# High and low activations side by side: the two matmuls that share weights take 320 and 256 columns instead of 288 and 288

## The reference

```python
h = _rmsnorm(x, norm_mix)
proj = h @ w_in                        # 2048 x 7240: q, k, v, indexer, S5 input u, two gates
attn = _dsa_attend(...)                # indexer scores, top-k, attention over selected keys
y_a = attn @ w_attn_proj
s5_y, new_re, new_im = _s5(u, ...)     # diagonal complex state-space scan
z = jax.nn.gelu(s5_y)
glu_a, glu_g = jnp.split(z @ w_glu, 2, axis=-1)
y_b = glu_a * jax.nn.sigmoid(glu_g)
x = x + (jax.nn.sigmoid(ga) * y_a + jax.nn.sigmoid(gb) * y_b) @ w_out
up = _rmsnorm(x, norm_ffn) @ w_up      # 2048 x 11264, then a causal conv of width 3
x = x + (jax.nn.silu(gate) * val) @ w_down
y = _rmsnorm(x, norm_final)
```

## Time and profile before

| | |
|---|---|
| runs | 1706.43, 1709.63, 1708.58 us; median 1708.58 |
| the profiled execution | 1707.09 us, of which 1705.4 us from the first to the last instruction |
| TensorE matmuls busy | 1622.1 us, 95% of the span, 12814 instructions |
| VectorE busy | 1026.1 us, 60% |
| ScalarE busy | 771.1 us, 45% |
| GpSimd busy | 457.1 us, 27% |
| DMA queues | 274.46 MB, mean 161 GB/s |

### The profile page before, as it was taken

How to read it: one execution, slowest core, us unless ns; L and a number is a source line. 1 busy time by engine, 2 the same in 40 slices (tenths; PEclk the granted TensorE clock), 3 DMA queues, 4 the chain that set the end, 5 groups by cost and what they waited for, 6 DMA issues and landing times.

```text
span 1705.4 us, 35779 instructions
## 1 busy us (share of the span) xinstructions
PE 1622.1 (95%) x12814; PEld 1588.9 (93%) x12814; DVE 1026.1 (60%) x1542; ACT 771.1 (45%) x1082; POOL 457.1 (27%) x650
## 2 busy tenths in 40 slices
PE   6699989889998999999999999999999999999997
PEld 4699879889898999999999999999999999999997
DVE  4574465757465555666677777777777774444441
ACT  4233434455455665343445445445445444333333
POOL 2591256664642332012211111111111112000110
PEclk9799899999999999999999999999999999999998
DMA  7355425445446555755564554554555556555552
GB/s 247 111 146 165 122 81 150 138 126 165 138 141 216 154 163 146 208 168 159 193 197 148 159 185 149 159 183 153 158 181 156 157 179 231 165 166 169 161 170 73
DMA packets 278087, 274.46 MB, mean 161 GB/s; under 512 B 21979, under 2 KB 275031, under 8 KB 276912
## 3 DMA queue, kind: packets, MB, share of 16 engines
q1 hardware_dynamic: 266128, 247.37, 47.7%
q10 hardware_dynamic: 9024, 18.23, 3.1%
q0 software_dynamic: 2848, 7.64, 1.3%
HBM read 259.56 MB, written 13.60 MB: 160 GB/s over the span
## 4 chain that ended last, share of the span: by engine, by line
PE 77%; POOL 6%; DVE 5%; ACT 4%; issue 4%; DMA 1%; ACTq 1%; POOLq 1%; SPq 0%; DVEq 0%
PE banks L417 24%; PE banks L419 24%; PE banks L418 24%; PE banks L425 2%; POOL clam L1630 2%; DVE wlo L1046 2%; ACT tlag L847 1%; POOL wq L1603 1%; DMA raw<-in_w_in 1%; POOL clam L1462 1%; ACT whi L739 1%; DVE sc L1162 1%; DMA scratch_mask<-wks 1%; POOL xb L1652 1%; POOL xs L1662 0%
## 5 line engine op out<-in xcount | busy, mean ns | idle before, releaser
L1046 DVE TENSOR_TENSOR wlo<-raw,whi 128x1024 fp32r<-128x1024 f32 x444 | 554.3, 1262 | 343.0 <-ACT whi L739 337.6
L739 ACT ACTIVATE whi<-raw 128x1024 fp32r<-128x1024 f32 x444 | 462.5, 1052 | 490.5 <-PE banks L419 466.3
L418 PE MATMUL banks<-h_lo,whi 128*128 128x288 f32 x1408 | 415.7, 295 | 0.0
L419 PE MATMUL banks<-h_hi,wlo 128*128 128x288 f32 x1408 | 415.7, 295 | 0.0
L417 PE MATMUL banks<-h_hi,whi 128*128 128x288 f32 x1408 | 414.6, 294 | 0.1
L417 PE MATMUL banks<-hhi,whi 128*128 128x288 f32 (+1 forms) x928 | 283.0, 305 | 20.6 <-DVE wlo L1046 18.6
L419 PE MATMUL banks<-hhi,wlo 128*128 128x288 f32 (+1 forms) x928 | 278.5, 300 | 0.0
L418 PE MATMUL banks<-hlo,whi 128*128 128x288 f32 (+1 forms) x928 | 278.3, 300 | 0.0
L418 PEld LDWEIGHTS banks<-h_lo,whi 128*128 128x128 f32 x1408 | 264.6, 188 | 0.1
L417 PEld LDWEIGHTS banks<-h_hi,whi 128*128 128x128 f32 x1408 | 264.1, 188 | 0.3 <-issue 0.3
L419 PEld LDWEIGHTS banks<-h_hi,wlo 128*128 128x128 f32 x1408 | 264.4, 188 | 0.0
(11 more groups left out here) (355 smaller groups left out, 2432.0 us busy)
## 6 DMA issues: line engine op xcount, KB each, us to landing
raw<-in_w_up SPq DMA_DIRECT2D x352, 256.0 KB, 3.4
raw<-in_w_in SPq DMA_DIRECT2D x224, 256.0 KB, 3.2
raw<-in_w_down SPq DMA_DIRECT2D x176, 256.0 KB, 3.0
raw<-in_w_glu SPq DMA_DIRECT2D x64, 256.0 KB, 2.9
raw<-in_w_out SPq DMA_DIRECT2D x64, 256.0 KB, 3.2
raw<-in_w_attn_proj SPq DMA_DIRECT2D x32, 256.0 KB, 4.1
scratch_gates<-gt ACTq DMA_DIRECT2D x16, 288.0 KB, 3.2
x<-scratch_x_kept ACTq DMA_DIRECT2D x2, 2304.0 KB, 9.2
```

Source lines behind the costliest of these rows:

```text
L418: pe.matmul(out, h, xl[:, kt, :], start=False, stop=False)
L419: mm = pe.matmul(out, lo, xh[:, kt, :], start=False, stop=kt == nk - 1)
L739: act.activation(whi[:, s, :, 0:cols], raw[:, s, :, 0:cols], ACT.Copy).then_inc(hi_ready, 1)
L1046: dve.tensor_tensor(wlo[:, s, :, 0:cols], raw[:, s, :, 0:cols], whi[:, s, :, 0:cols], ALU.subtract).then_inc(lo_ready, 1)
```

## The change

**Layout.** Each pair of buffers becomes one of [128, tiles, 576]: low half in columns 0 to 287, high half in 288 to 575. In a tile the order is then low prompt (256), low samples (32), high prompt (256), high samples (32). Addresses of the whole are as before; `z` tiles are stored rotated by four, because of what else lies there, and read in the same order as before (`k0=4`).

**Matmuls.** The first with the high weights now reads 320 columns, low samples and the whole high half, into columns 0 to 319 of the bank; the second the 256 low prompt columns into 32 to 287; the third, with the low weights, the 288 high columns into 32 to 319. The result (`res`) lies in columns 32 to 319, but the products of the low samples lie apart, in columns 0 to 31 (`extra`).

**VectorE.** Before each use of a group, `add_extra` copies the 2 x 32 extra columns to SBUF (`part`) and adds them to the sample columns of the result, in PSUM; `fold` is `add_extra` with a link behind it. The KIWI group has the same by halves, four instructions.

**GLU gate.** ScalarE's sigmoid of the gate half (L922) read the accumulator by itself, behind `acc_free[0]`; it now waits for `gate_folded`, which VectorE gives after it has waited for the group and added.

```diff
+    part = at("part", [P, 2, TS], F32, 4960)
...
-    hhi = at("hhi", [P, KD, T], F32R, RE)
-    hlo = at("hlo", [P, KD, T], F32R, RE + 18432)
+    hx = at("hx", [P, KD, 2 * T], F32R, RE)
+    hlo, hhi = hx[:, :, 0:T], hx[:, :, T:2 * T]
...
+    res, extra = acc[:, :, TS:TS + T], acc[:, :, 0:TS]
...
-                            out = acc[0:w, 2 * g_parity + m, 0:T]
+                            out = acc[0:w, 2 * g_parity + m, :]
...
-                            pe.matmul(out, h, xh[:, kt, :], start=kt == 0, stop=False)
-                            pe.matmul(out, h, xl[:, kt, :], start=False, stop=False)
-                            mm = pe.matmul(out, lo, xh[:, kt, :], start=False, stop=kt == nk - 1)
+                            xk = x[:, (k0 + kt) % nk, :]
+                            pe.matmul(out[:, 0:TS + T], h, xk[:, TP:2 * T], start=kt == 0, stop=False)
+                            pe.matmul(out[:, TS:TS + TP], h, xk[:, 0:TP], start=False, stop=False)
+                            mm = pe.matmul(out[:, TS:TS + T], lo, xk[:, T:2 * T], start=False, stop=kt == nk - 1)
...
-                    act.wait_ge(acc_free[0], 15 + i)
-                    act.activation(glu_gate[:, :, :], acc[:, 2:4, 0:T], ACT.Sigmoid).then_inc(acc_free[1], 1)
+                    act.wait_ge(sem("gate_folded"), i + 1)
+                    act.activation(glu_gate[:, :, :], res[:, 2:4, :], ACT.Sigmoid).then_inc(acc_free[1], 1)
...
+            def add_extra(parity):
+
+                samples = res[:, 2 * parity:2 * parity + 2, TP:T]
+                own.link(dve.tensor_copy(part[:, :, :], extra[:, 2 * parity:2 * parity + 2, :]))
+                return dve.tensor_tensor(samples, samples, part[:, :, :], ALU.add)
+
+            def fold(parity):
+                own.link(add_extra(parity))
+
             def evac(dst, parity, c_end):
 
                 dve.wait_ge(chunks_used, c_end)
-                dve.tensor_tensor(dst, acc[:, 2 * parity:2 * parity + 2, 0:T], bc(rstd[:, :], 1, 2), ALU.mult).then_inc(acc_free[parity], 1)
+                fold(parity)
+                dve.tensor_tensor(dst, res[:, 2 * parity:2 * parity + 2, :], bc(rstd[:, :], 1, 2), ALU.mult).then_inc(acc_free[parity], 1)
...
+                    dve.wait_ge(chunks_used, c + 2)
+                    add_extra(1).then_inc(sem("gate_folded"), 1)
                     lo(c, 4)
```

More of the change, by code:

```diff
@@ L401, in _, with group @@
         def _(pe):
-            def group(g_parity, use, c, nk, xh, xl, widths=(P, P), before={}, slot0=0):
+            def group(g_parity, use, c, nk, x, widths=(P, P), before={}, slot0=0, k0=0):
                 if not (isinstance(use, int) and use == 0):
@@ L452, in _ @@
             mm.then_inc(sem("rb_ready"), 1)
[L453 to L460, removed]
+            group(1, 0, C_U + 4, KD, hx)
+            group(0, 1, C_U + 8, KD, hx)
+            group(1, 1, C_U + 12, KD, hx)
+            group(0, 2, C_KIWI, KD, hx, widths=(P, IH))
+            group(1, 2, C_QI, KD, hx)
+            group(0, 3, C_QI + 4, KD, hx)
+            group(1, 3, C_KV, KD, hx)
+            group(0, 4, C_KV + 4, KD, hx)
             for r in range(4):
@@ L572, in gates @@
                 more = it < N_GATE - 1
[L573 to L574 removed]
+                group(1, 6 + it, c, KD, hx, before={0: (lambda: chunk_inputs(it),), 2: ahead})
+                group(0, 7 + it, c + 4, KD, hx, before={0: (lambda: powers_t(it + 1, 0),), 1: (lambda: powers_t(it + 1, 1),),
                                                               2: (lambda: lag_kernels(it + 1),)} if more else {})
@@ L654, in unit @@
                     start = ()
-                group(1, 14 + i, c, 8, zhi, zlo, before={0: start, 1: middle})
-                group(0, 15 + i, c + 2, 8, zhi, zlo, slot0=2, before={0: (lambda: prompt_probs(i),),
+                group(1, 14 + i, c, 8, zx, k0=4, before={0: start, 1: middle})
+                group(0, 15 + i, c + 2, 8, zx, slot0=2, k0=4, before={0: (lambda: prompt_probs(i),),
                                                                       1: (lambda: prompt_values(i), lambda: sample_probs(i))})
@@ L1095, in evac_blocks @@
                 dve.wait_ge(chunks_used, C_U + 4 * k + 4)
+                fold(k % 2)
                 for i in range(4):
@@ L1120, in _ @@
             dve.wait_ge(chunks_used, C_KIWI + 4)
-            dve.tensor_tensor(kiT[:, :], acc[:, 0, 0:T], rstd[:, :], ALU.mult)
-            dve.tensor_tensor(wiT[:, :], acc[0:IH, 1, 0:T], rstd[0:IH, :], ALU.mult).then_inc(acc_free[0], 1)
+            own.link(dve.tensor_copy(part[:, 0, :], extra[:, 0, :]))
+            own(dve.tensor_tensor(res[:, 0, TP:T], res[:, 0, TP:T], part[:, 0, :], ALU.add))
+            own.link(dve.tensor_copy(part[0:IH, 1, :], extra[0:IH, 1, :]))
+            own.link(dve.tensor_tensor(res[0:IH, 1, TP:T], res[0:IH, 1, TP:T], part[0:IH, 1, :], ALU.add))
+            dve.tensor_tensor(kiT[:, :], res[:, 0, :], rstd[:, :], ALU.mult)
+            dve.tensor_tensor(wiT[:, :], res[0:IH, 1, :], rstd[0:IH, :], ALU.mult).then_inc(acc_free[0], 1)
             for k, (dst, par) in enumerate(((qiT[:, 0:2, :], 1), (qiT[:, 2:4, :], 0), (kT[:, :, :], 1))):
@@ L1299, in _ @@
             with loop("DVE", 0, 4) as turn:
-                own.loop(turn, 16)
+                own.loop(turn, 22)
                 for u in range(2):
@@ L1344, in _ @@
             with loop("DVE", 0, N_PROJ) as it:
+                own.loop(it, 4)
                 for s in range(2):
@@ L1371, in _ @@
                     ins.then_inc(sem("h2_ready"), 1)
+            own.done(N_OUT)
             dve.wait_ge(sem("sum_ready"), 1)
@@ L1409, in _ @@
             with loop("DVE", 0, N_UP) as it:
-                own.loop(it, 14)
+                own.loop(it, 18)
                 c = C_UP + 8 * it
```

72 lines of the change are left out of this document (39 added, 33 removed).

## The result

The changed kernel takes 1718.72 us, the median of five runs (1704.14 to 1723.36); the kernel before, measured with it, 1707.87 us (1705.56 to 1709.63). The ratio is 1.0052, with a 95% interval of 1.0029 to 1.0076: slower by half a per cent. The profiled execution took 1723.36 us.

The account below looks back on a forecast made before the run. TensorE's own pace was taken as the bound: TensorE 0, uncovered folds 4.2 + 1.8 + 1.5 + 0.5 = 8.0 us on 1708.6 gave 1716.6 us, range 1642 to 1723 us.

Parts of the forecast that it names:

- TensorE, 0 us: Matmul triples of 320, 256 and 288 columns take 397.8 ns as before, so no change; bounds -66 and +41 us.
- steps of 64: Rival: TensorE takes columns in steps of 64, so a triple falls from 15 steps to 14; 1651 us, chance 0.28.
- a short one without gain: Rival: the 256-column matmul still takes 132.6 ns while the long one pays its 32 columns; 1758 us, chance 0.09.
- the 12.6 ns: Time on top of 120 ns for a 288-column matmul at full clock, read as a steady price per matmul or column.
- DOWN within 1 us of 280: Sign in the profile after: the forecast is wrong if DOWN's length moves by more than 1 us from 280 us.
- The fold, 0.54 to 0.6 us: VectorE's copy and add of 0.23 us each, with two links of 0.04 us; 0.75 us in a hardware loop.
- Where it counts, 8.0 us: Folds on the way to something TensorE waits for: GATE 4.2, U, KV and Q 1.8, loops 1.5, end 0.5 us.
- OUT to UP: Between these stages `x`, then GpSimd's squares, then TensorE wait behind a fold in a loop: 0.75 us.
- Q: The fold before `qT`, which leads to the head sums and the next `lo`, delays TensorE by 0.6 us.
- the forecast's ring: GATE's cycle from one `gt` to the next, 33.7 us, is lengthened by a fold 7 times: 7 x 0.6 = 4.2 us.
- UP, covered: In UP 44 folds, 33 us, fit VectorE's idle time and cost nothing; 33 us if that cover were gone.
- The gate's new wait: In GLU it comes when VectorE has only the next `lo` to do, which waits for ScalarE anyway: 0.

Follow-up runs that it names:

- e3_folds: e1_layout plus the gate's new wait and 113 folds of the same size that change no value; 1714.93 us, ratio 1.0038 to the kernel before.
- e1_layout: Changed kernel's common buffers and result columns 32 to 319, but three matmuls of 288 columns and no folds; 1702.02 us, 0.9967 to the kernel before.
- e2_widths: Changed kernel's buffers and widths 320, 256, 288 without folds, the gate's wait the old one; 1704.39 us, 0.9989 to the kernel before.
- e8_widths_again: e2_widths run once more unchanged, for a second profile; 1703.98 us, ratio 0.9985 to the kernel before.
- e9_split384: Changed kernel with matmuls of 384 and 192 columns instead of 320 and 256, folds of 2 x 96; 1783.28 us, 1.0460 to the kernel before.

## Why the prediction came out right, point by point

Forecast 1716.6 us; measured 1718.72 and 1715.47. The time holds, the sum behind it only in part: terms were missing that mostly cancel, the stall (+5 us), the buffers (-6 us) and perhaps the widths (+3 to 4 us). That the sum came out within 2 us is luck, and the stated range of 1642 to 1723 us is too wide to bear out any one mechanism; the distances between starts do that.

- **TensorE, 0 us.** Right in form: 320, 256 and 288 columns at 2.4 GHz (133.3, 106.7, 120 ns) and 13.3 to 13.5 ns on top of each in the first profile; neither steps of 64 nor a short one without gain. Wrong was to take the 12.6 ns as a constant of the matmul. It goes with where the tiles of x lie, and, with the new buffers and widths, with the execution (393.3 to 400.0 ns per triple). The N/2.4 + 2.5 ns that the forecast quotes is, on that page, the gap of a matmul by itself and not of a stream; no term of the sum used it. The trace of before could show only the one value that its layout gives. Without folds, the new buffers and widths together are 2 to 3 us faster than before by the medians (0.9989 and 0.9985), though both intervals take in no change. The buffers give 6 (0.9967, 0.9962), clear of noise; that the widths take some 3 to 4 of it is the difference of the two, and not shown by itself. The test in the forecast, DOWN within 1 us of 280, failed both ways: from its first start to its last it was 280.4 us before, 281.5 in the first profile and 277.1 in the second.
- **The fold, 0.54 to 0.6 us.** 0.52 us; copy 222 ns, add 232 ns.
- **Where it counts, 8.0 us.** All folds cost 12.9 us (`e3_folds` against `e1_layout`) or some 11 (changed kernel against `e2_widths` and `e8_widths_again`). 5 to 6 of these are the stall at the entry of UP. The 6 to 7 that remain are near the 8.0. Four places are shown, each by its own rows: U 0.5, OUT to UP 0.5, UP to DOWN 0.5 and the end 0.5 us, 2.1 together, where the forecast had 0.6, 0.75, 0.75 and 0.5, 2.6 together. Q is 0.9 by the means (forecast 0.6). GATE, half of the forecast, is not shown: 5 us by the mean of four profiles (forecast 4.2), but nothing in `e9_split384` and in the run with GATE's folds alone, which speaks against the forecast's ring. The ring of 34.3 us is met by the mean of seven in the first profile (34.3, before 33.9) and passed in the second (34.8).
- **UP, covered.** Right for the folds, which never hold TensorE there once the loop runs. The step that failed is the list of what an added instruction costs: its time on the engine was counted, and not that it moves the program behind it. The test in the forecast, no new waits in UP, failed by this one, 3.33 us.
- **GLU.** The gate's new wait was taken as 0. The stage is 165.4 to 166.2 us in the four profiles with all folds (`e9_split384`, with its slower matmuls, apart) and 162.8 to 165.4 in the nine without them: 1.6 us by the means, against a spread of 2.6. So some of it may be the fold or the wait; no run has either alone.

## What to carry to other kernels

Columns may be moved from one matmul to another at little or no price only as long as each still covers a load of weights (288, 256: yes; 192: no). Where a kernel stands at TensorE's pace, look first at how the moving tiles lie: here both halves in one buffer, with 2304 bytes from tile to tile instead of 1152, made the kernel 0.3 to 0.4% faster, with the same matmuls. And an instruction added to an engine's program can cost more by where it pushes a loop's entry than by its time: look for instruction transfers and an unexplained gap at the loops behind it, and try a few more or fewer instructions before calling the idea slow.

## What was not expected of the hardware

- The pace of three fp32r matmuls with 864 columns in all, at the 2.4 GHz level, takes one of a few values (393.3, 396.7, 398.3, 400.0 ns, which at 2.4 per ns are 944, 952, 956 and 960 clocks, 80 to 96 over the columns), fixed through a stage, and with the new buffers and widths different from one execution to another. The Trainium skill (TensorE: Matmul & The Clock Gate, Back-to-back issue gap) has, for a matmul by itself, 2.5 ns on top of the columns, where the stream of these rows has 11.1 to 13.3; at the 1.2 GHz level the rows agree with its N/1.2.
- At one position of VectorE's program the entry of a loop, with two transfers of instructions at that time, stopped VectorE for 3.3 us. TensorE, which stood still for 3.33 us behind it, then ran at granted clock 0.50 for 3.4 us, which cost 1.7 us more.
